# A two-layer diffusion step: value projection ahead of queries and keys, with the loads of the dot pieces reordered

## The reference, cut to what matters

```
sm, cm, gm, sf, cf, gf = split(silu(cond) @ w_ada[1] + b_ada[1], 6)
h = x * (1 + cm) + sm
q, k, v = split(h @ na_w_qkv + na_b_qkv, 3)
new_k, new_v = k, v of the prompt tokens
x = layer_norm(ALPHA * x + gm * (attention(q, k, v) @ na_w_out + b), ln_g[1, 0], ln_b[1, 0])
```

## Time and profile before

| | us |
|---|---|
| median of 3 runs | 1075.79 |
| lowest and highest | 1075.53, 1077.47 |
| the profiled execution's own time | 1074.48 |
| span of the profiled execution | 1072.6 |
| mean granted clock of TensorE, share of full speed | 0.973 |

### The profile page before, as it was taken

One profiled execution on the slowest core, in us unless ns is written; L12 is line 12 of the kernel. 1 busy time (PEld: TensorE's weight loads), 2 busy tenths in 40 slices (PEclk: granted clock), 3 DMA queues, 4 the chain that ended last, 5 costly groups with the idle time before them and its releaser, 6 DMA issues.

```text
span 1072.6 us, 25713 instructions
## 1 busy us (share of the span) xinstructions
PE 1012.6 (94%) x10500; PEld 608.3 (57%) x10500; DVE 596.8 (56%) x1399; ACT 208.5 (19%) x499; POOL 324.1 (30%) x429
## 2 busy tenths in 40 slices
PE   8999999999889999999989999999988999999983
PEld 2545555565556666666555554566455666666651
DVE  6448996874743333333479992475665333333336
ACT  4152223002310000000150000363231000000002
POOL 1400000510145555544300000155013555554442
PEclk9999999999899999999989999799999999999997
DMA  9964467371999999999998788433078899999991
GB/s 332 401 237 156 177 242 293 113 280 67 352 399 405 406 405 405 352 405 406 370 395 287 263 323 303 128 100 98 0 267 356 306 405 406 395 385 404 405 384 64
DMA packets 101690, 318.48 MB, mean 297 GB/s; under 512 B 8402, under 2 KB 12690, under 8 KB 101235
## 3 DMA queue, kind: packets, MB, share of 16 engines
q1 hardware_dynamic: 91716, 299.13, 72.8%
q0 software_dynamic: 5776, 17.30, 4.7%
q10 hardware_dynamic: 4128, 1.05, 0.4%
HBM read 311.70 MB, written 5.77 MB: 296 GB/s over the span
## 4 chain that ended last, share of the span: by engine, by line
PE 77%; DVE 8%; DMA 5%; SPq 4%; ACT 2%; issue 2%; POOL 2%; DVEq 0%; ACTq 0%
PE bank L771 74%; DMA ring<-in_moe_w_down 4%; SPq L501 4%; POOL P L745 1%; PE bank L1216 1%; DVE st L1977 1%; DVE P L2037 1%; DVE hT L1752 1%; DMA row_beta<-in_ln_b 1%; ACT x L1378 1%; PE bank L972 0%; DVE x L1778 0%; DVE x L2082 0%; PE bank L830 0%; DVE sc L1808 0%
## 5 line engine op out<-in xcount | busy, mean ns | idle before, releaser
L771 PE MATMUL bank<-ring,xgT 128*32 128x256 f32 x4224 | 241.3, 380 | 2.1 <-issue 1.6
L771 PE MATMUL bank<-hT,ring 128*128 128x384 f32 x640 | 208.8, 489 | 2.1 <-DVE hT L1752 2.1
L771 PEld LDWEIGHTS bank<-ring,xgT 128*32 128x32 f32 x4224 | 145.7, 110 | 79.4 <-issue 4.2
L1942 DVE TENSOR_TENSOR he<-sa,bank 128x128 f32<-128x128 f32 x66 | 19.0, 288 | 286.6 <-ACT sa L1424 286.6
L771 PEld LDWEIGHTS bank<-hT,ring 128*128 128x128 f32 x640 | 122.1, 191 | 88.3 <-issue 5.2
L1574 DVE CUSTOM_DVE_ANT_0 ring<-ring,ring 128x1024 f32<-128x1024 f32 x120 | 146.8, 1223 | 3.5
L771 PE MATMUL bank<-ring,heT 128*32 128x256 f32 x2112 | 129.2, 385 | 4.2 <-DMA ring<-in_moe_w_down 4.2
L771 PE MATMUL bank<-yg,ohT 32*128 32x256 f32 x1632 | 107.3, 391 | 3.1 <-DVE yg L1971 2.9
L725 POOL TENSOR_TENSOR yg<-ysb,gate_s 128x256 f32<-128x256 f32 x128 | 91.0, 732 | 42.5 <-ACT ysb L1429 42.4
L771 PEld LDWEIGHTS bank<-ring,heT 128*32 128x32 f32 x2112 | 63.3, 110 | 60.1 <-issue 27.0
L771 PEld LDWEIGHTS bank<-yg,ohT 32*128 32x128 f32 x1632 | 74.6, 184 | 36.0 <-issue 26.4
(11 more groups left out here) (284 smaller groups left out, 1107.7 us busy)
## 6 DMA issues: line engine op xcount, KB each, us to landing
ring<-in_moe_w_up SPq DMA_DIRECT2D x64, 2048.0 KB
ring<-in_moe_w_down SPq DMA_DIRECT2D x32, 2048.0 KB
ring<-in_k_ada SPq DMA_DIRECT2D x15, 2048.0 KB
ring<-in_w_ada SPq DMA_DIRECT2D x9, 2048.0 KB
ring<-in_na_w_qkv SPq DMA_DIRECT2D x6, 2048.0 KB
ring<-in_hy_w_in SPq DMA_DIRECT2D x5, 2048.0 KB
ring<-in_hy_w_out SPq DMA_DIRECT2D x2, 2048.0 KB
ring<-in_na_w_out SPq DMA_DIRECT2D x2, 2048.0 KB
```

The source lines that it names most:

```text
L771: return nc.tensor.matmul(out, lhsT, rhs, start=first, stop=last)
L1942: v.tensor_tensor(he[:], sa[:], ps[0][:, 128:256], ALU.mult).then_inc(S["he_ready"], 1)
```

## The change

It alters the order of work at the start of layer 1, on five engines.

- TensorE turns tiles 0 and 1, then makes the first value group (tile 0, `qkv_4`), then turns tile 2, then makes the other five value groups, and then the 16 groups of q and k. Each value group waits for the evictions of its own tile alone. Each half of `kctx` now waits for the evictions of its four blocks of kT.
- SP requests `qkv_4` first, then `sb1`, then ln_g and ln_b, then `dot1_4`, `qkv_5`, and the other dot pieces among q's and k's weights. Slots change with the order.
- VectorE applies ln_g and ln_b to tile 0 before it modulates tile 2. It evacuates value groups before q, with seven of the dot rows between them, then q with two rows behind each, then nine rows at the end.
- ScalarE's code has only the new group numbers: it modulates tile 2 when that is turned, so its `silu` of `sb1` comes later, and it stores `new_v` after the last k eviction.
- GpSimd requests `bv` after the last combine of the first MoE, ahead of `kctxT` and `vctx`, on a semaphore of its own (`bv_in`).

```
-              "sb1", "qkv_0", "dot1_4", "dot1_5", "qkv_1", "dot1_6", "dot1_7", "qkv_2", "dot1_8", "dot1_9", "qkv_3", "dot1_10", "dot1_11",
-              "qkv_4", "qkv_5", "out1", "moe1"]
+              "qkv_4", "sb1", "dot1_4", "qkv_5", "dot1_5", "dot1_6", "qkv_0", "dot1_7", "dot1_8", "qkv_1", "dot1_9", "dot1_10", "qkv_2",
+              "dot1_11", "qkv_3", "out1", "moe1"]
+VALUE_ROWS = [0, 0, 1, 3, 5, 7, 7]
...
-                  ... ("xm1_0", 2), ("xm1_1", 2), ("xm1_2", 2), ("qk", 16), ("v", 6), ("kctx", 2), ...
+                  ... ("xm1_0", 2), ("xm1_1", 2), ("v0", 1), ("xm1_2", 2), ("v", 5), ("qk", 16), ("kctx", 2), ...
...
+def value_group(n):
+
+    return G_AT["v"] + n - 1 if n else G_AT["v0"]
...
-                if name == "qkv_1":
+                if name == "dot1_4":
                     rows_after_experts(0)
...
+            pool.wait_ge(acc_ready, 1)
+            row_to_all(bv[:], A["na_b_qkv"][:, 2 * D:3 * D], D).then_inc(bv_in, 16)
             pool.wait_ge(ln_done, TT * 2)
...
-            row_to_all(bv[:], A["na_b_qkv"][:, 2 * D:3 * D], D).then_inc(att_in, 16)
...
             turn_tile("xm1_1", x_block, 1)
-            pe.wait_ge(norm_done, 2 * TT + 6)
-            turn_tile("xm1_2", x_block, 2)
-            for t in range(TT):
-                for h in range(2):
-                    wait_evacuated(pe, G_AT[f"xm1_{t}"] + h)
+            for h in range(2):
+                i = W_AT[f"qkv_{4 + h}"]
+                wait_weights(pe, i)
+                w = w_view(i, 8, 512)
+                for t in range(TT):
+                    for half in range(2):
+                        wait_evacuated(pe, G_AT[f"xm1_{t}"] + half)
+                    out = bank(value_group(TT * h + t))
+                    for k in range(KT):
+                        last = mm(out[:, :], hT[:, k, t * 128:(t + 1) * 128], w[:, k, :], k == 0, k == KT - 1)
+                    last.then_inc(group_ready, 1)
+                    if h == 0 and t == 0:
+                        pe.wait_ge(norm_done, 2 * TT + 6)
+                        turn_tile("xm1_2", x_block, 2)
             for s in range(4):
...
                 for j in range(4):
+                    wait_evacuated(pe, G_AT["qk"] + KT + 4 * h + j)
                     last = nc.tensor.transpose(out[:, j * 128:(j + 1) * 128], kT[:, 4 * h + j, 0:128], ident[:])
...
             modulate_lower("xm1_1", 1, 0, 8, 1)
-            modulate_lower("xm1_2", 1, 0, 8, 2)
             dve.wait_ge(rows_moe_in, 32)
             for t in range(TT):
+                if t == 1:
+                    modulate_lower("xm1_2", 1, 0, 8, 2)
                 wait_group(dve, G_AT[f"xm1_{t}"] + 1)
                 affine_g(t, rows_moe)
                 affine_b(t, rows_moe[:, 2, :])
+            dve.wait_ge(bv_in, 16)
+            for n in range(6):
+                g = value_group(n)
...
+                v.tensor_tensor(tok[:, t, hs], ps[bank_of(g)][:, :], bv[:, hs], ALU.add).then_inc(evacuated[g % 8], 1)
+                for r in range(*VALUE_ROWS[n:n + 2]):
+                    dot_row(1, r)
...
-                for r in (2 * j, 2 * j + 1):
+                for r in (VALUE_ROWS[-1] + 2 * j, VALUE_ROWS[-1] + 2 * j + 1):
                     dot_row(1, r)
-            for r in range(2 * KT, DOT_ROWS[1]):
+            for r in range(VALUE_ROWS[-1] + 2 * KT, DOT_ROWS[1]):
                 dot_row(1, r)
```

More of the change, by code:

```diff
@@ L96 @@
                   ("inv", 8), ("gm0", 4), *ending(0),
-                  ("cond7", 1), ("cond8", 1), ("cond7_sum", 1), ("cond8_sum", 1), ("xm1_0", 2), ("xm1_1", 2), ("xm1_2", 2), ("qk", 16), ("v", 6), ("kctx", 2), ("gm1a", 2), ("gm1b", 2), *ending(1)]:
+                  ("cond7", 1), ("cond8", 1), ("cond7_sum", 1), ("cond8_sum", 1), ("xm1_0", 2), ("xm1_1", 2), ("v0", 1), ("xm1_2", 2), ("v", 5), ("qk", 16), ("kctx", 2), ("gm1a", 2), ("gm1b", 2), *ending(1)]:
     G_AT[_name] = _at
     _at += _n
+def value_group(n):
+    return G_AT["v"] + n - 1 if n else G_AT["v0"]
 APART = {G_AT[f"cond{k}{part}"]: k - 7 for k in (7, 8) for part in ("", "_sum")}
@@ L370, in build @@
         evacuated = [sem(f"evacuated{b}") for b in range(8)]
-        first_in, x_in, filt_in, rows_in, rows_moe_in, moe_in, att_in, dft_in, skip_in, skip_ready = (
-            sem(n) for n in ("first_in", "x_in", "filt_in", "rows_in", "rows_moe_in", "moe_in", "att_in", "dft_in", "skip_in", "skip_ready"))
+        first_in, x_in, filt_in, rows_in, rows_moe_in, moe_in, att_in, bv_in, dft_in, skip_in, skip_ready = (
+            sem(n) for n in ("first_in", "x_in", "filt_in", "rows_in", "rows_moe_in", "moe_in", "att_in", "bv_in", "dft_in", "skip_in", "skip_ready"))
         scond_ready, mod_ready, scond_zero = sem("scond_ready"), sem("mod_ready"), sem("scond_zero")
@@ L461, in last_group @@
                     if j == W_AT[f"qkv_{s}"]:
-                        return G_AT["qk"] + 4 * s + 3 if s < 4 else G_AT["v"] + TT * (s - 4) + TT - 1
+                        return G_AT["qk"] + 4 * s + 3 if s < 4 else value_group(TT * (s - 4) + TT - 1)
             def wait_slot_free(i):
@@ L1185, in _ @@
             wait_all_evacuated(pe, G_AT["out1_00"])
-            pe.wait_ge(att_in, 48)
+            pe.wait_ge(att_in, 32)
             units = TT * PAIRS
@@ L1478, in _ @@
                                      bias=VT[:, V_BQK + KT + j:V_BQK + KT + j + 1]).then_inc(evacuated[g % 8], 1)
-            for g in (G_AT["v"], G_AT["v"] + TT):
+            for g in (value_group(0), value_group(TT)):
                 wait_evacuated(act, g)
@@ L1998, in _ @@
                 affine_b(t, rows_moe[:, 2, :])
+            dve.wait_ge(bv_in, 16)
+            for n in range(6):
+                g = value_group(n)
+                h, t = divmod(n, TT)
+                hs = slice(h * 512, (h + 1) * 512)
+                wait_group(dve, g)
+                v.tensor_tensor(tok[:, t, hs], ps[bank_of(g)][:, :], bv[:, hs], ALU.add).then_inc(evacuated[g % 8], 1)
+                for r in range(*VALUE_ROWS[n:n + 2]):
+                    dot_row(1, r)
             for j in range(KT):
@@ L2010, in _ @@
             v.memset(credit[:, 4:5], 0.0).then_inc(mod_ready, 1)
[L2011 to L2017, removed]
             for c, name in enumerate(("gm1a", "gm1b")):
```

## The result

| | before | changed |
|---|---|---|
| median, us (9 runs each) | 1076.49 | 1079.47 |
| lowest and highest | 1073.41, 1077.49 | 1078.08, 1080.97 |
| ratio to before | | 1.0029 [1.0015, 1.0043] |
| span of the profiled execution | 1072.6 | 1077.3 |

What follows compares the result with a forecast made beforehand. TensorE bounds the kernel, matmuls busy 94% of the span, so only its idle or low-clock time can be won. Terms -2.6 + 0.9 + 0.0 + 0.5 = -1.2 us, applied to the median 1075.79, gave 1074.6; range 1072.2 to 1077.4.

Steps and rivals of the forecast that it cites:

- The start of the value projection: Layer 1: the first value group needs tile 0 alone, so it starts at 547.35, 2.6 us earlier (bounds 2.1 and 3.0).
- Turning tile 2: Its eight transposes now stand between two value groups: 0.9 us added at full clock, upper end 2.0.
- The clock at the start: Value projection: full clock returns 3.1 us after dense work begins, as before; no difference, bounds 0.4 less and 1.3 more loss.
- Rival (a): The clock keeps its own moments at projection and attention: +1.3 and +0.6, net +0.7, 1076.5 us; chance 0.17.
- Third tile, bv, rows, Silu, weights: Projection: tile 2, bias and norm rows, ScalarE's Silu and the weight loads all arrive in time; zero each.
- Rival (c): Projection: a weight, at qkv_2, is late because a dot row frees its slot; +3.2, 1079.0 us; chance 0.11.
- moe1's later requests: The second MoE's second and third weight pieces wait for the last dots but are used after attention; zero.
- The end of the projection: The second half of kT's turning waits for the last eviction: 0.5 us added, bounds 0.2 and 0.8; new_v's store covered.
- Attention's clock: Prompt units drive the low clock, so its return moves with the work: zero; up to 0.6 us given back otherwise.
- Rival (b): The clock returns much sooner in attention's prompt units: -2.5, and 0.4 at the projection; together -4.1, 1071.7 us; chance 0.17.
- What comes after: Attention, output projection and second MoE are ordered by events behind the change and shift along, with no added time.

Runs made afterwards that it cites:

- the early store alone: The changed kernel, but ScalarE requests new_v's store before the first k eviction, some 40 us ahead of new_k's; ratio 0.9997 to before.
- The run without rows among the values: The changed kernel with new_v's store requested before the first k eviction and no dot rows between the value evictions; ratio 1.0325 to before.
- the fillers: Two unread matmuls, before the first and behind the second scores; added to the changed kernel with new_v's store before the first k eviction: ratio 0.9953 to before.
- the four filled kernels without the held request: Two unread matmuls added to before (0.9976) and, with new_v stored early, to the changed kernel (0.9953), tile 2 turned first (0.9946), all tiles waited for (0.9974).
- tile 2 first: Changed kernel, new_v stored early, tile 2 turned before the first value group, each group waiting for its own tile; 0.9988, with two unread matmuls 0.9946.
- The two without the head start: Changed kernel, new_v stored early, tile 2 turned first and all three tiles waited for; ratio 1.0017 to before, with two unread matmuls 0.9974.
- the old order with the store late: The kernel before, with new_v's store requested directly ahead of new_k's and nothing else changed; median 1080.95 us, ratio 1.0048.

## Why the prediction was wrong

**The start of the value projection (-2.6).** Right: 2.8 us sooner.

**Turning tile 2 (+0.9).** Right: 0.87.

**The clock at the start (0.0).** Mis-sized on both sides: the bounds were 0.4 less and 1.3 more, the profiles show 1.6 less and 1.4 more. (The row at 553 puts the return at 553.14 and not 553.07, since its 0.93 mixes the levels 1.0 and 0.5; that changes no term.) From the first projection matmul to the turning of kT the changed kernel took 124.7 us (the clock back before it, no loss), the early store alone 127.7 (back at 554.0, 6.0 us after the start), the kernel before 125.4 and 126.9. Over the six profiles that start as the changed kernel does, the clock was back 1.2 to 2.3 us ahead of the first projection matmul in four and 6.0 to 6.2 us behind it in two; with the old order it was back 3.1 to 3.2 us behind it in three and 6.2 in one. The Trainium skill (TensorE: Matmul & The Clock Gate, Part 1) had it that the monitor does not restart with the work, and the traces agree: one and the same piece of code met the clock at 1.2 GHz for its first 6.0 us and at 2.4 GHz from its first matmul. Rival (a)'s first half did occur, in some executions.

**Third tile, bv, rows, Silu, weights (zero each).** Right: no wait for a weight; qkv_1 was requested at 596.7 where I had 599.6, qkv_2 at 619.1 where I had 622.6. Rival (c) did not happen. The run without rows among the values shows that a weight can be late in this order, first of all qkv_1. That (c)'s 1079.0 lies beside the measured 1079.47 is chance.

**moe1's later requests (zero).** Wrong in what it left out. They keep the transfers going until 685, while the two stores are under way.

**The end of the projection (+0.5).** The added wait cost 0.1 us (1.00 from kT to the gates, 0.88 before). The step that failed stands in the same paragraph of the prediction: "ScalarE has the new_v store (0.4) on top, but its next user on the path, the first exponential, stands behind the gates and the first scores, which take TensorE some 5 us more, so that is covered." I priced the request at its own 0.43 us and looked only at what follows it. What it pushes together was not looked at: new_k's request, the next on the same queue, 1.7 us behind it instead of 14.6. Its hold was 7.29 us, of which some 3 lay under ScalarE's wait for the first maximum; 4.0 came through. In the medians the move of that one request was worth 3.4 us, and 9 with the fillers in, where the early store also keeps the clock. The profile of before shows no hold, but it did show both requests, their packets and their distance. The Trainium skill (DMA: Bandwidth & Descriptors, Issuing engines are not separate DMA queues) calls the time on the sequencer that starts a DMA "usually small relative to the DMA itself"; here it was 0.38 us or 7.29 for the same instruction, depending on what was pending.

**Attention's clock (zero).** I took it that the prompt units themselves drive the clock down. The fillers show that the two idle times of a microsecond ahead of them have a large part in it: in three of the four filled kernels without the held request the same units ran at full clock in the profile. In the fourth, with tile 2 first, the clock fell all the same, so they are not the only cause. Rival (b) had the right price for a unit at full clock, 1.4 us (measured: first scores of successive units at 681.87 and 683.25), but I put it down to luck.

**What comes after (shifts along).** Doubtful by the profiles. From the first expert matmul of the second MoE to the end of the span the four profiles of the old order took 253.9 to 254.2 us, and the nine of the new one (without the run that has no rows among the values) 253.7 to 257.1, eight of them 254.6 or more, 255.6 in the mean. The two without the head start are among the slower ones, so it isn't the head start. Those 1.5 us are more than the whole gain that I forecast; but the medians of the filled kernels (0.9974 without the head start, 0.9976 before) show nothing of them, so the difference isn't established. Of a cause I can say only that in the first pair TensorE's waits for moe_w_down grew by the same 1.6 us; over all profiles the two do not go together (the old order with the store late waited 5.7 us and took 254.2).

**Range and side.** 1079.47 lies outside 1072.2 to 1077.4, whose lower end is also further out than the "halfway to (b)" that I wrote (1073.2). The slower side was given to the weights alone; ScalarE's queue was never on the list of what could be late.

What stays open is whether the hold is set by the number of packets, their size, or their sum with the other traffic; new_k's store on another engine's queue was not tried. It also stays open whether the second MoE takes longer in the new order, and why.

## What to carry to other kernels

When a step is moved, look at every request on its engine's queue before and after, and at the distance to the next one there: a store of 2048 small packets held the next request on that queue, and all behind it, for 5 to 7 us here. Request stores as soon as their data are there. Where a stage of small matmuls follows a dense one, look at the granted clock and at the idle times of a microsecond between them; an unread matmul in each was worth 2.6 to 4.7 us in the median here where no longer wait followed, and the best kernels (0.9953 and 0.9946) are the changed one with an early store and these two lines, the second with tile 2 turned first.

## What the runs showed of the hardware that I had not expected

- A store's request took 0.38, 5.52, 6.60, 7.13 or 7.29 us on ScalarE, by how far the earlier store on the same queue had come: in the four held cases it was let go at 64% to 66% of that store's time to landing (11.2 to 19.1 us). With 6.8 us between the requests it was still held for 5.52.
- The clock stayed low for 13.6 to 24 us through units that kept TensorE over 90% busy by the profile, and in three profiles of the four filled kernels without the held request it stayed at full speed through the same units once two gaps ahead of them were filled.
- One and the same kernel differed by up to 8 us between executions (before: 1072.1 to 1080.4 over the jobs), with low stretches of the clock at other moments. A single profile is then no measure of a change of 0.2%: the first profile of before was 2 us under its own median.
